# Second stage of the first MLP: feature tiles requested one group of four earlier, and weights requested ahead of the conditioning transfers

## What is computed

```
def _squared_relu_mlp(h, w1, w2):
    a = jax.nn.relu(h @ w1)
    return (a * a) @ w2          # a: 1024 tokens x 4096 features, w2: 4096 x 1024

def ada_mod(cond, w, b):         # for c and for c_ctx
    m = jax.nn.silu(cond) @ w + b    # w: 1024 x 6144
    return jnp.split(m, N_MOD, axis=-1)
```

## Time and profile before

| | us |
|---|---|
| median of 3 runs (2860.65 to 2862.29) | 2862.2 |
| the profiled execution, its own time | 2854.34 |
| span of its trace | 2852.5 |
| PE busy in the span | 2730.2 (96%) |
| DVE busy | 1428.3 (50%) |
| ACT busy | 964.0 (34%) |

### The profile page before, as it was taken

One profiled execution on the slowest core, in us unless ns is written; L12 is line 12 of the kernel. 1 busy time (PEld: TensorE's weight loads), 2 busy tenths in 40 slices (PEclk: granted clock), 3 DMA queues, 4 the chain that ended last, 5 costly groups with the idle time before them and its releaser, 6 DMA issues.

```text
span 2852.5 us, 41120 instructions
## 1 busy us (share of the span) xinstructions
PE 2730.2 (96%) x17452; PEld 2278.2 (80%) x17452; DVE 1428.3 (50%) x1900; ACT 964.0 (34%) x1487; POOL 177.5 (6%) x153
## 2 busy tenths in 40 slices
PE   8999998999999788899799999999999999999999
PEld 7887887878888677777789878877787888888887
DVE  6445454476656566555535565565635333333332
ACT  5445444444444111126332443344523111221111
POOL 2112122100000000005100000000000000000000
PEclk9999999999999899999899999999999999999999
DMA  4110110413334555442323221121711111111111
GB/s 129 44 35 29 38 39 24 118 40 110 116 112 148 184 188 180 174 173 83 107 82 125 65 71 57 38 77 38 284 52 44 45 52 45 52 45 52 48 49 67
DMA packets 225094, 246.67 MB, mean 86 GB/s; under 512 B 8464, under 2 KB 188176, under 8 KB 224912
## 3 DMA queue, kind: packets, MB, share of 16 engines
q1 hardware_dynamic: 224912, 244.04, 26.2%
HBM read 205.21 MB, written 38.80 MB: 86 GB/s over the span
## 4 chain that ended last, share of the span: by engine, by line
PE 64%; DVE 6%; DMA 6%; ACT 4%; issue 2%; SPq 1%; POOL 1%; DVEq 0%; ACTq 0%; POOLq 0%
PE ps L510 6%; PE ps L513 6%; PE ps L526 6%; DMA a_r<-a_scratch 5%; PE ps L888 4%; PE ps L879 4%; PE ps L881 4%; PE ps L806 3%; PE ps L808 3%; PE ps L810 3%; PE ps L1064 2%; PE ps L1065 2%; PE ps L1069 2%; PE ps L596 2%; PE ps L592 2%
## 5 line engine op out<-in xcount | busy, mean ns | idle before, releaser
L1911 DVE TENSOR_TENSOR Wlo<-Wraw,Whi 128x1024 fp32r<-128x1024 f32 x184 | 229.5, 1253 | 747.0 <-ACT Whi L1362 747.0
L1362 ACT ACTIVATE Whi<-Wraw 128x1024 fp32r<-128x1024 f32 x196 | 205.7, 1056 | 1028.9 <-PE ps L526 336.2
L510 PE MATMUL ps<-Hh,Whi 128*128 128x512 f32 x912 | 284.4, 393 | 0.0
L513 PE MATMUL ps<-Hh,Wlo 128*128 128x512 f32 x912 | 281.9, 390 | 0.0
L592 PE MATMUL ps<-Whi,Hh 128*128 128x256 f32 x768 | 223.3, 291 | 8.1 <-ACT Hh L1393 8.1
L596 PE MATMUL ps<-Whi,Hl 128*128 128x256 f32 x768 | 220.0, 286 | 8.0 <-DVE Hl L1941 8.0
L526 PE MATMUL ps<-Hl,Whi 128*128 128x512 f32 x912 | 225.4, 395 | 0.2 <-issue 0.2
L594 PE MATMUL ps<-Wlo,Hh 128*128 128x256 f32 x768 | 218.7, 285 | 0.0
L838 PE MATMUL ps<-a_h,Whi 128*128 128x512 f32 x512 | 162.2, 399 | 46.7 <-ACT a_h L1574 46.7
L513 PEld LDWEIGHTS ps<-Hh,Wlo 128*128 128x128 f32 x912 | 171.8, 188 | 36.3
L879 PE MATMUL ps<-ah,Whi 128*128 128x512 f32 x512 | 199.3, 389 | 0.6 <-ACT ah L1625 0.6
(11 more groups left out here) (351 smaller groups left out, 5128.7 us busy)
## 6 DMA issues: line engine op xcount, KB each, us to landing
Wraw<-in_m_w SPq DMA_DIRECT2D x96, 512.0 KB, 4.0
n<-in_w_ada SPq DMA_DIRECT2D x64, 512.0 KB, 4.0
Wraw<-in_w_in SPq DMA_DIRECT2D x56, 512.0 KB, 4.1
pair<-in_m_w SPq DMA_DIRECT2D x32, 512.0 KB, 5.3
a_scratch<-ub SPq DMA_DIRECT2D x64, 256.0 KB, 2.0
a_r<-a_scratch SPq DMA_DIRECT2D x32, 512.0 KB, 5.8
R<-in_xT SPq DMA_DIRECT2D x16, 512.0 KB, 4.8
Wraw<-in_w_gate SPq DMA_DIRECT2D x16, 512.0 KB, 4.1
```

What stands on the lines that cost most here:

```text
L510: e.matmul(t[:, c], wh[:, k, ms], opd.hi[:, k, c], start=k == 0, stop=False)
L513: e.matmul(t[:, c], wl[:, k, ms], opd.hi[:, k, c], start=False, stop=False)
L1911: e.tensor_tensor(Wlo[n % 4][:], Wraw[n % 2][:], Whi[n % 4][:].bitcast(F), ALU.subtract).then_inc(*S("w_lo", "v").tick(n))
```

## The change

Only SP's list is changed: the same requests in another order. Tiles 4 to 7 are requested before the stage; in the stage `a_load` is called for tile 4i+8+jw in place of 4i+4+jw. Two conditioning steps are requested ahead of the loop, so that SP's steps are two further on than VectorE's at the same product. And the weight tile of pair jw is requested at the even product, before that product's conditioning steps, in place of at the odd one, behind its steps.

```diff
             for s in range(len(SEQ) - AHEAD, len(SEQ)):
                 quarter_out(s)
+            for t in range(4, 8):
+                a_load(t)
...
+            modulation()
+            modulation()
             for i in range(8):
                 for m in range(8):
+                    if m % 2 == 0:
+                        feed(upto((0, "s2", i, m // 2)))
                     if i < 7:
                         for _ in range(1 + (m % 4 == 0)):
                             modulation()
-                    if m % 2:
-                        feed(upto((0, "s2", i, m // 2)))
-                        if i < 7:
-                            a_load(4 * i + 4 + m // 2)
+                    if m % 2 and i < 6:
+                        a_load(4 * i + 8 + m // 2)
```

## The result

| | us |
|---|---|
| kernel before, median of 7 runs (2858.53 to 2862.51) | 2860.89 |
| changed kernel, median of 7 runs (2851.03 to 2854.66) | 2852.82 |
| ratio | 0.9970, 95% interval 0.9959 to 0.9982 |
| profiled execution of the changed kernel, its own time | 2853.6 |
| span of its trace | 2851.7 |

The change gains 8.1 us; 11.7 us were forecast.

The account below looks back on a forecast made before the run. The prediction took the ring of weight tile and conditioning step, not PE, as the stage's clock. Five groups -9.3, start -2 and end -0.4 sum to -11.7 us: 2862.2 to 2850.5 us, own range 2843 to 2856, eight in ten 2836 to 2865.

Parts of the forecast that it names:

- third landing: Weight, third of three 512 KB transfers, lands 6.5 us after the first request (bounds 6.2 and 7.35).
- The ring: Weight lands, `Whi`, `Wlo`/`a_l`, addition, conditioning step, SP's conditioning and weight requests: turns of 11.1 and 13.7 us.
- `Whi` to SP's request in 5.8 us: In each turn, from the begin of `Whi` to SP's conditioning request: 5.8 us, where it was 5.97.
- Intervals alike: Successive `Whi` begin near 12.4 us apart (5.8 + 6.5 + 0.1), in place of 11.1 and 13.7.
- step 49: Conditioning step whose request waits for one step instead of two steps back: 2.3 us extra, before as after.
- Floor of a group's first turn: At a group's start ACT needs the buffer PE frees with its second product: turn not below about 12.05 us.
- Start, -2 us: Start of the stage: first restart at 966.5 to 968.4 us against 969.63, taken as -2 us.
- Behind the last stop, -0.4: After the last stop, one weight tile is requested ahead of the context's transfer: 0 to -1, taken as -0.4 us.
- A: Rival: third place costs the weight little, landing 4.7 us behind its own request; 2833 us, chance 0.08.
- B: Rival: PE's stops vanish with the half pace behind them, some 59 us; 2803 us, chance 0.03.
- C: Rival: nothing to be measured, third landing 6.75 to 7.25 us, gain under 5.7 us; 2861 us, chance 0.19.
- D: Rival: slower, the request itself stalls as in a 1.99 us feature request, third landing 7.35 us; 2870 us, chance 0.12.

Follow-up runs that it names:

- Tiles alone: Kernel before with tiles 4 to 7 requested ahead of the stage and `a_load` one group further, conditioning steps and weights as they were: 2852.89 us, ratio 0.9992.
- the four traces: Four single traced executions of the changed kernel, no edit, beside four of the kernel before: mean span 2849.1 us against 2853.5.
- weight-second kernel: Changed kernel with the weight request exchanged with the feature tile's, both still behind the odd product's conditioning request: 2810.87 us, ratio 0.9840.

## Why the prediction came out as it did

The time was forecast at 2850.5 us and is 2852.8. What bounds the stage, what the change does to it and why it gains so little came out as forecast. The gain did not in size: 11.7 us forecast, 8.1 and 6.3 measured, since the term of the third landing was too small. In the order of its steps:

- **The ring is the bound, not late feature tiles: right.** Tiles alone gave 3.2 us; exchanging two requests gave 38.
- **`Whi` to SP's request in 5.8 us: right,** 5.82.
- **Intervals alike: right; 12.4 us: too low.** This is the step with the largest error: *"I take 6.5"* for the third landing. Leaving out the 2.3 us of step 49, the fifteen turns that don't begin a group have means of 12.8, 12.6, 12.5 and 12.7 in the four traces, 12.7 over all, so the landing is 12.7 - 5.9 = 6.8 us, and 7.0 in the turn shown. Read from the transfers themselves, 86 in the four traces, it is 6.7 us on average. I had added the gaps of one step and one median to the requests as they stood before; the third of three now lands 5.6 to 6.1 us behind its own request (medians 5.8, 5.8, 5.6 and 5.7), a few 7.1. The whole stage: 256.2 measured against 250.3 forecast, 0.3 us a turn.
- **The base: a little off the other way.** 259.64 us for five groups was the lowest of four traces of the kernel before; their mean is 261.4. That is 1.8 us given back, so that the term of -9.3 measured -5.2.
- **Floor of a group's first turn, 12.05 us: wrong,** without much effect. It took the half pace behind a restart as it was. It lasts longer in the changed kernel, and first turns are 12.2 to 13.5 us; in the first trace the ones ending at 978.07, 1185.95 and 1237.21 were held by PE's buffer, not by the weight. They average 12.8 over the four traces, against the forecast's 12.4.
- **Seven stops: right; one to a group: not quite; 4 us each: too low.** Six groups have stops, and the first of them has two, before as after: 2.1 and 11.7 us, then one each of 4.5 to 6.5.
- **Start, -2 us: right in sign,** -1.0 of the means, within their scatter.
- **Behind the last stop, -0.4: wrong in sign,** +1.8. The rows above show where half of it comes from: from the restart to the product after next PE takes 11.20 us (1236.95 - 1225.75), where it was 9.87 (1239.14 - 1229.27), and the means of four traces are 10.9 and 10.0. The context's transfer is asked for later by the same 0.9 us (49.1 against 48.3 us behind the sixth restart, means of four). The other 0.9 us is not settled.
- **The 7.9 us between the profiled execution and the runs: right for the kernel before, not for the changed one.** The forecast puts the changed kernel's profiled execution at 2842.6 us; it took 2853.6, 0.8 us above the median of its runs. The first trace of the kernel before (2854.34 us) lies below all seven of its runs and near those of the later sets (medians 2855.56 and 2856.07). Why is not known. The forecast of the runs' time starts from their own median and does not suffer by it.

Sum of the measured terms: -1.0 - 5.2 + 1.8 = -4.4 us, where the medians of runs give 8.1 in the first set and 6.3 in the second. Four spans of a kind lie 4.7 and 4.8 us apart, so their means are uncertain by about 1 us each, and the 95% intervals of the two ratios reach from 5 to 12 and from 3 to 8 us, so the readings are not far enough apart to be at odds; the runs, more in number, decide the size, and the traces the place.

**The rivals.** A (third place costs little, 2833) is refuted by the landings, 5.8 and not 4.7 us; its price for the *second* place is what the weight-second kernel has. B (stops vanish, 2803) is not this change, but its condition was the right one: with the weight request free of its own turn's step, the kernel gains 60.3 us where B had 59. C had as its condition a third landing of 6.75 to 7.25 us on average, and the average is 6.8 or 6.7, by the two readings above: on C's lower edge. Its time did not come: the base was 1.8 us higher than I took it, and the gain lies just above C's bound of 5.7 us. By its landing the change stands between the forecast and C. That its time fell to the forecast is in part luck: the traces' terms make 4.4 of the 11.7 us. D (slower, 7.35) did not occur: 0.43 us for the feature request where it feared 1.99. Of what *would show it*, the kinds came and the sizes were missed: turns of 12.4 us by 0.3, weight transfers of 5.5 to 5.7 us by 0.1 in two of four medians, stops of about 4 us by up to 2.5 behind the first group, and 49.6 us between restarts by 1.6 (256.2 / 5 = 51.2, where the forecast's 250.3 / 5 is 50.1 with step 49).

What the prediction did not see is how little separated the change from a much better one. It said that the odd product's step still stands ahead of the weight and that the weight is third, and took both as given. Undoing the first, which here also made the weight second in its row, was worth 54 us (-60.3 against -6.3, each against the kernel before on its chip), undoing the second alone 38.

## What to carry to other kernels

- Where an engine waits for a transfer, look at what stands ahead of the request in the issuing queue, and what that waits for: if it is a consumer of the same transfer, there is a ring, and one turn of it, added up from rows, is the stage's clock. Asking earlier for what the waiting engine *names* gave 3 us of 60 here.
- In an in-order queue, a transfer that nobody awaits should stand behind the one that closes the turn: its place among three was worth 1.65 us a turn, and 38 us in all. A lead given to requests that wait for their own consumer is not free; it can put a wait ahead of everything behind them.
- Two transfers behind one wait make two rings. Freeing one of them gave -3.2 and +4.0 us here, moving both -34.

## What the runs showed of the hardware

- **A shorter stop can be followed by longer half pace.** Behind a stop of 6.35 us the third pass of the restarted product takes 2.72 us, behind one of 4.54 us 3.62 us, at full pace 1.98. In the four traces of each kernel it is 2.6 to 3.0 before and 3.4 to 3.6 after, at that same restart. From the restart to the product after next it is 9.87 us (1239.14 - 1229.27) against 11.20 (1236.95 - 1225.75): 1.3 of the 1.8 us by which the stop was shortened came back; by the means of four traces it is 0.9 of 1.4 us. Where the stops go there is nothing to give back: the weight-second kernel has one of 2.28 us from 966 to 1228 us, and its clock there is 1.00.
- **Three transfers of 512 KB asked for within 0.9 us** land 3.6, then about 1.3 and 2.1 us apart in the step shown (36.17 + 3.6, 36.54 + 4.5, 37.07 + 6.1), and the third landing scatters from 6.2 to 8.3 us behind the first request. The average of a trace, 6.6 to 6.9 us over some 21 turns, is most of the difference between the changed kernel's executions in this stage, 253.5 to 258.8 us.
